# Constant matmuls on TensorE ahead of its waits between the stages of a two-stack transformer kernel

## The reference, cut to what matters

```python
x = x + rms_norm(y @ w_out[l], norm_post[l])
x = x + jax.nn.sigmoid(x @ w_ple_gate[l]) * (p[l] @ w_ple_proj[l])
```

```python
x = x + rmsnorm(m, norm_mix_post[layer])
f = conv_ffn(rmsnorm(x, norm_ffn_pre[layer]), ...)
x = x + rmsnorm(f, norm_ffn_post[layer])
```

## Time and profile before

| | us |
|---|---|
| median of 3 runs | 3065.9 |
| lowest and highest | 3062.34 and 3066.22 |
| the profiled execution, its own time | 3065.92 |
| its span, first to last instruction | 3064.1 |
| PE busy | 2972.2 (97%) |
| DVE busy | 1852.6 (60%) |
| POOL busy | 1117.8 (36%) |
| ACT busy | 1060.3 (35%) |
| mean granted TensorE clock | 0.987 |

### The profile page before, as it was taken

The page is one execution under the profiler, slowest core; times in us unless marked ns, Lnnn a source line. Parts: engine busy times, 40 slices in busy tenths (PEclk is TensorE's granted clock), DMA queues, the critical chain, the costliest instruction groups (busy, mean ns, idle before and its releaser), DMA issues.

```text
span 3064.1 us, 38689 instructions
## 1 busy us (share of the span) xinstructions
PE 2972.2 (97%) x15272; PEld 2361.3 (77%) x15272; DVE 1852.6 (60%) x3007; ACT 1060.3 (35%) x1875; POOL 1117.8 (36%) x468
## 2 busy tenths in 40 slices
PE   8999999999999999899999999998999999899998
PEld 6777778877777778777778778886788878678886
DVE  4865565556755655635553598615767676588832
ACT  4443342344433432433323322224333333422221
POOL 3323334343233334333333344443333333244442
PEclk9999999999999999999999999999999999999999
DMA  5222223232222223222222233332222222223332
GB/s 192 79 81 66 73 73 100 83 96 69 83 63 74 76 92 97 93 72 76 83 83 83 76 94 99 97 97 79 83 77 75 77 76 77 63 76 97 97 99 73
DMA packets 78328, 260.20 MB, mean 85 GB/s; under 512 B 10730, under 2 KB 13546, under 8 KB 78148
## 3 DMA queue, kind: packets, MB, share of 16 engines
q1 hardware_dynamic: 77572, 255.63, 26.6%
q10 hardware_dynamic: 576, 2.10, 0.2%
HBM read 255.53 MB, written 6.09 MB: 85 GB/s over the span
## 4 chain that ended last, share of the span: by engine, by line
PE 88%; DVE 7%; ACT 2%; DMA 1%; issue 1%; POOL 1%; SPq 0%; ACTq 0%; DVEq 0%
PE bank L672 26%; PE bank L674 25%; PE bank L673 25%; PE bank L787 2%; PE bank L834 2%; PE bank L814 1%; PE bank L992 1%; DVE x_res L1762 1%; PE bank L703 1%; PE bank L1028 1%; DMA bias_copies<-bias_vectors 1%; PE bank L793 1%; PE bank L1066 1%; POOL w_lo L539 1%; DMA w_raw<-in_w 0%
## 5 line engine op out<-in xcount | busy, mean ns | idle before, releaser
L539 POOL TENSOR_TENSOR w_lo<-w_raw,w_hi 128x1024 fp32r<-128x1024 f32 x458 | 1113.8, 2434 | 1891.6 <-ACT w_hi L1173 1891.6
L672 PE MATMUL bank<-h_hi,w_hi 128*128 128x512 f32 x2784 | 1126.7, 405 | 46.4 <-DVE h_lo L1750 20.4
L674 PE MATMUL bank<-h_hi,w_lo 128*128 128x512 f32 x2784 | 1093.6, 393 | 0.0
L673 PE MATMUL bank<-h_lo,w_hi 128*128 128x512 f32 x2784 | 1092.7, 393 | 0.0
L1173 ACT CAST w_hi<-w_raw 128x1024 fp32r<-128x1024 f32 x458 | 479.2, 1048 | 1253.0 <-PE bank L674 1234.8
L672 PEld LDWEIGHTS bank<-h_hi,w_hi 128*128 128x128 f32 x2784 | 527.6, 190 | 179.8 <-issue 59.9
L674 PEld LDWEIGHTS bank<-h_hi,w_lo 128*128 128x128 f32 x2784 | 526.9, 189 | 114.9
L673 PEld LDWEIGHTS bank<-h_lo,w_hi 128*128 128x128 f32 x2784 | 528.6, 190 | 101.0 <-issue 0.3
L2027 DVE TENSOR_SCALAR m<-bank,gains 128x512 f32<-128x512 f32 x48 | 36.1, 751 | 310.6 <-ACT ta L1371 186.9
L1304 ACT ACTIVATE probs<-probs,small_columns 128x128 f32<-128x128 f32 (+2 forms) x192 | 101.9, 531 | 175.2 <-DVE small_columns L1805 171.0
L674 PE MATMUL bank<-f_hi,w_lo 128*128 128x512 f32 x352 | 136.9, 389 | 0.0
(11 more groups left out here) (279 smaller groups left out, 3695.5 us busy)
## 6 DMA issues: line engine op xcount, KB each, us to landing
w_raw<-in_w SPq DMA_DIRECT2D x458, 512.0 KB, 3.5
bias_copies<-bias_vectors SPq DMA_DIRECT2D x1, 2560.0 KB
x_res<-in_x_t ACTq DMA_DIRECT2D x4, 512.0 KB, 8.0
bias<-bias_copies SPq DMA_DIRECT2D x8, 256.0 KB, 3.4
bias<-bias_copies SPq DMA_DIRECT2D x16, 128.0 KB, 2.4
out_x<-x_res SPq DMA_DIRECT2D x8, 256.0 KB, 2.0
bias_copies<-bias_vectors SPq DMA_DIRECT2D x1, 1280.0 KB
ple_raw<-in_p_t SPq DMA_DIRECT2D x2, 512.0 KB, 3.7
```

The costliest lines, as they stand in the source:

```text
L539: pool.tensor_tensor(WL[slot][:], RAW[slot][:], WH[slot][:].bitcast(F32), ALU.subtract).then_inc(sems["lo_done"], 1)
L672: pe.matmul(banks[bank][:], WH[slot][:, w], hi[:, k, :], start=start, stop=False)
L673: pe.matmul(banks[bank][:], WH[slot][:, w], lo[:, k, :], start=False, stop=False)
L674: pe.matmul(banks[bank][:], WL[slot][:, w], hi[:, k, :], start=False, stop=stop).then_inc(sems["kt_done"], 1)
```

## The change

A new method `busy` waits until a bank's last content has been read, and multiplies `ID` by `ONES` into the first 128 columns of that bank n times. Nothing reads the result: the next real matmul there starts a new sum. `BEHIND_PLE` is 26. The calls are: 26 at the start of `mix` for layer 1 and of `retention`; 4 in `linear` between the two column sums (6 linear layers); 3 at the end of `linear` (all but the last, 5); 12 in `ffn_up` behind the spread (2); 15 in `dilated` behind the spread (1). That makes 130 matmuls in all. DVE, ACT, POOL and SP have the same programs as before.

```diff
+BEHIND_PLE = 26
@@ class Programs of PE
+                def busy(self, n, bank=None):
+
+                    bank = self.rot % ROTATION if bank is None else bank
+                    if bank in self.last:
+                        name, value = self.last[bank]
+                        pe.wait_ge(sems[name], value)
+                    for _ in range(n):
+                        pe.matmul(banks[bank][:, 0:P], ID[:], ONES[:], start=True, stop=True)
@@ mix
+                    if l:
+                        self.busy(BEHIND_PLE, 0)
                     first = [self.open(b) for b in (5, 6, 7)]
@@ linear
                     self.column_sums(OUTB, TC, last=False)
+                    self.busy(4)
                     pe.wait_ge(sems["m_squared"], t.at("m_squared"))
                     self.column_sums(OUTB, TB, first=False).then_inc(sems["summed"], t.one("summed"))
+                    if self.stage < N_STAGES - 1:
+                        self.busy(3)
@@ ffn_up
                     self.spread(OUTB)
+                    self.busy(12)
                     t.up("operand", KT)
@@ dilated
                     self.spread(OUTB)
+                    self.busy(15, DIL_FIRST_BANKS[0])
                     t.up("operand", KT)
```

## The result

The change made the kernel slower: a median of 3070.02 us (14 runs, 3067.28 to 3072.81) against 3062.21 us (14 runs, 3060.57 to 3066.22) for the kernel before. The ratio is **1.0022, 95% interval 1.0014 to 1.0030**. The ratios in this text are estimated together with their intervals and are not the quotients of the medians (here 7.8 us apart, or 1.0026); amounts in us beside a ratio are worked out from the ratio, so here 6.7 us, with an interval of 4.3 to 9.2. The profiled execution took 3070.0 us, span 3068.2. That of the kernel before took 3065.92, in the upper part of its own runs: the two spans differ by 4.1 us, the medians by 7.8.

A forecast was written before the change was run, and what follows sets the result against it. PE, busy 2972.2 of 3064.1 us, was taken as the bound, leaving idle time and a lowered clock to win. 8.2 + 0.5 + 1.4 - 2.9 = +7.2 us on 3065.9 gave 3073.1 us, range 3063 to 3081.

The forecast's parts named there:

- The barrier: Ahead of mix1 and ret: added matmuls wait for DVE's end of the previous stage, leaving 1.87 of 6.87 us.
- The 26: Behind each ple stage: 8.4 us, 6.6 late; less 5.0 saved on plain matmuls, +8.2 us for both.
- R: Time from the restart of dense work to the clock's return behind a ple stage, taken as 5.3 us.
- Price: One added float32 matmul, priced from attention-value rows: two records, 0.223 us at full clock, 0.43 at half.
- rival (c): Constant matmuls don't raise the clock, so the 26 behind ple run at half clock: 3091 us; chance 0.06.
- (a): Added matmuls are hidden in the wait behind ple and hold the clock: 3059.9 us; chance 0.10.
- (b): Each added matmul is one record, 0.11 us, so the whole takes 3066.3 us; chance 0.10.
- The ple starts: At 586.78 and 1222.03 the clock stays up through the spread: -1.3 and -1.6 us.
- hides 0.4: Behind mix0, mix1, ffn0 and dil ACT's table load hides 0.4 of the 0.62 us drain delay: +0.2 each.
- The 3 at the other barriers: Behind the column sums they delay the barrier: ret +0.6 us, ffn0 and dil +0.2 each; +1.4 over all five.
- The 12 and 15: Behind the spreads of ffn_up and dilated: DVE paces the operands, so zero; bound 0 to +1.5 us in all.
- The last 4: Between the last linear layer's column sums: push the end by 0.9 us, about 0.4 beside ACT's table load: +0.5.

The follow-up runs named there:

- The 104: The change with 52 constant matmuls in place of 26 at each of the two places: 3083.49 us against 3063.58 for the kernel before, ratio 1.0067.

## Why the prediction was right

- **The barrier** was the step that decided, and it held. ACT starts at 648.70 and PE at 648.83, both released by DVE's queue. PE's room was 1.74 of the 6.9 us; the forecast had 1.87, because it took ACT's start for PE's, which comes 0.13 later.
- **The 26**: forecast 8.4 us each in place, 6.6 late, 5.0 saved over both. Measured 8.41 and 8.40, 6.7 late at both, 4.9 saved, so 8.5 against the forecast 8.2. The working also holds inside: 8.41 us is what 52 records give if the clock comes back 5.5 us after the restart (25.7 records at 0.213, the rest at 0.112). R was taken as 5.3.
- **Price**: 0.223 us a matmul was taken from the attention-value rows. In the change's trace the records start 0.112 us apart at full clock and 0.213 at half, two for each matmul: the forecast's numbers. The 104 against 52 records give 0.235 and 0.22. By the 56 ns that the Trainium skill gives for an isolated matmul of 128 columns (TensorE: Matmul & The Clock Gate, section Back-to-back issue gap) each would have cost a quarter of that, and the trace doesn't agree for these float32 operands; with the four passes that its page FP8 and Floating Point Precision (section TensorE Precision Notes) counts for true float32, it does.
- **The clock does come back under constant matmuls**: rival (c), 0.06, is out. So are (a) and (b): the records start behind the barrier, and there are two for each matmul.
- **The ple starts**: forecast -2.9 and +0.4 for the 3, measured -4.0 and +1.3. Each term was too small, and they nearly cancel: -2.5 against -2.7. In ple1 the gain was 2.7 rather than 1.6, because at half clock six more plain matmuls behind the spread had run slowly too, which the sum stopped short of. The 3 cost 0.7 and 0.6 instead of 0.2 each: this step of the sum was too small by half a microsecond each time. Its "hides 0.4" is right for DVE and not for PE. DVE is indeed released only 0.3 us later (586.54 - 582.58 = 3.96 behind the start of the last plain matmul, 3.67 before), but PE's first plain matmul now starts 0.4 behind DVE's step where both had started together. Why PE takes these 0.4 after its own drain wasn't tried.
- **The 3 at the other barriers**: behind ret DVE's L1639 comes 0.7 us later (3.97 behind the last plain matmul against 3.27; 0.6 was forecast), released by PE's queue, and behind ffn0 and dil 0.3 later (0.2 was forecast). With the 0.4 of PE at both ple starts that adds up to about 2.7 us over the five, against the forecast's 1.4. The row behind ret (before: the earlier trace rows):

```profile
1719.42 0.16 DVE L1639 TENSOR_SCALAR small_columns<-bank 128x4 f32<-128x4 f32 x1 [1.08 <-PEq L634]
```

- **What held the clock at the ple starts**: the forecast argued it from the one wait of 2.50 us that brought no fall. The clock did stay up, and the experiments with and without the 3 bear the step out; but the premise was a lucky draw, since behind the same wait the clock fell in nine of 24 cases.
- **The 12 and 15**: forecast zero. With and without them the stretches of ffn0 and dil agree within 0.1 us in the traces and that of ffn1 within 0.4, so the reason given holds.
- **The last 4**: forecast +0.5, measured +0.8 in the change's trace. Counted from the last plain matmul, versions with it end 0.3 or 0.8 us later than the kernel before, and the three that leave it out and keep the other five 0.1 later: so it costs 0.2 to 0.7.
- **The sum**: 3073.1 was forecast from a median of 3065.9 of three runs, a ratio of 1.0023; measured 1.0022. That it fits so closely is partly luck: the interval is 0.0008 wide on either side, and two terms were off by 1.1 and 0.9 us in opposite directions. The absolute 3070.0 is lower because the median of before is 3062.2 with more runs. The lower bounds of the terms add up to 3071 and not to 3070. Slower by over 0.2% had 0.59, and 0.22% came out, with an interval of 0.14 to 0.30%: slower is shown, slower by over 0.2% is not.

## What to carry to other kernels

Before an idle engine is given filler work, look for what releases its first instruction there, not for what releases the first useful one: a wait of 6.9 us that the trace puts down to an operand was a barrier of 5.1 us and an operand wait of 1.7 us. Filler behind the barrier was paid for beyond these 1.7 us, filler ahead of it was free as long as it ended before the barrier did. Filler is also worth something only where other work waits for the engine it warms: where another engine paces the work, a full clock changes nothing. And the filler should be priced from rows of its own data type; a float32 matmul of 128 columns costs here as much as a plain one of 512.

## What the runs showed of the hardware that wasn't expected

- A matmul of identity and ones, whose result nobody reads, brings the granted clock back as real ones do: in the change's trace it returns 5.5 us after the restart, within the 52 records (6.1 us with plain matmuls before). It holds it up as well: with 20 ahead of the barrier and 4 behind it the clock is 1.00 at both boundaries.
- An idle stretch of 2.41 us let the clock fall twice in one execution, while one of 2.50 inside ffn0 did not the earlier trace rows. The same wait of 2.50 us, in the same work, was followed by a fall in 9 of 24 cases. With 0.68 and 0.60 us the clock stayed up. The length of the wait alone doesn't say what the clock does here.
- In eight of the ten experiments' profiles there are one or two further falls in mix0 or mix1, most of them 3.4 us long and worth some 1.5 us each, at places where the kernel before and the changed one have none. Six of them start near 120 us and five near 755, within about 2 us of the same matmul each, with no wait of PE over 0.1 us in the 6 us ahead. What sets them off stays open.
